# Moving the streamed operands of a 256-token block kernel to other places modulo 512 bytes

## The reference, cut to what matters

```python
# first block
xn = rms_norm(h, norm1_g)
proj = xn @ w_in                                 # 1024 -> 5136, cut into twelve pieces
for n, y in enumerate((y_a, y_b, y_c, y_d)):     # each (256, 512), made from the pieces
    merged += sigmoid(xn @ w_gate[n] + b_gate[n]) * (y @ w_branch[n])
h = h + merged @ w_out
h = h + square(relu(rms_norm(h, norm2_g) @ w_ff1)) @ w_ff2         # 1024 -> 4096 -> 1024
h = h + sigmoid(rms_norm(h, norm3_g) @ w_ple_gate + b) * (p @ w_ple)
x = rms_norm(h, final_g)
# second block, shift/scale/gain from c @ ada_w
z = modulate(rms_norm_2(x, norm1_g), sh1, sc1) @ w_in + b_in       # 1024 -> 5640
merged = sigmoid(ga) * (ym @ p_mlstm) + sigmoid(gb) * (ya @ p_moba)
x = x + g1 * (merged @ w_out)
f = silu(h2 @ w_gate) * (h2 @ w_up)                                # 1024 -> 2816
x = x + g2 * (f @ w_down)
return rms_norm_2(x, normf_g)
```

## Time and profile before

| | us |
|---|---|
| median of 3 runs | 926.76 |
| lowest and highest | 924.8, 931.33 |
| the profiled execution | 926.27 |
| its span, first to last instruction | 925.0 |

### The profile page before, as it was taken

One profiled execution on the slowest core, in us unless ns is written; L12 is line 12 of the kernel. 1 busy time (PEld: TensorE's weight loads), 2 busy tenths in 40 slices (PEclk: granted clock), 3 DMA queues, 4 the chain that ended last, 5 costly groups with the idle time before them and its releaser, 6 DMA issues.

```text
span 925.0 us, 18432 instructions
## 1 busy us (share of the span) xinstructions
PE 896.8 (97%) x7356; PEld 869.6 (94%) x7356; DVE 729.2 (79%) x1146; ACT 565.3 (61%) x819; POOL 1.9 (0%) x9
## 2 busy tenths in 40 slices
PE   7999999999999999999999999999999999999995
PEld 6999989998999999999999989998989999999995
DVE  6778989979888899888965988968779885555554
ACT  7848366675576676654446778557685664445452
POOL 0000000000000000000000000000000000000000
PEclk9999999999999999999999999999999999999998
DMA  8766545556774789998855565553435656666641
GB/s 309 250 195 222 157 151 165 162 181 216 262 252 160 251 289 344 336 319 301 320 181 181 159 194 183 161 153 120 151 125 179 203 169 198 190 200 193 192 143 46
DMA packets 52533, 188.78 MB, mean 204 GB/s; under 512 B 5968, under 2 KB 6240, under 8 KB 52320
## 3 DMA queue, kind: packets, MB, share of 16 engines
q1 hardware_dynamic: 52304, 187.60, 61.4%
q10 hardware_dynamic: 144, 0.00, 0.0%
HBM read 186.53 MB, written 1.05 MB: 203 GB/s over the span
## 4 chain that ended last, share of the span: by engine, by line
PE 81%; DVE 12%; ACT 6%; issue 1%; DMA 0%; SPq 0%; DVEq 0%; ACTq 0%
PE bank L991 23%; PE bank L993 23%; PE bank L994 23%; DVE wlo L1024 3%; ACT whi L1817 2%; PE bank L965 1%; PE bank L967 1%; PE bank L966 1%; DVE cv L1098 1%; DVE hsc L1502 1%; DVE scr L1197 1%; PE bank L696 1%; ACT P L1928 1%; DVE stat L1229 1%; DVE Alo L1059 1%
## 5 line engine op out<-in xcount | busy, mean ns | idle before, releaser
L1024 DVE TENSOR_TENSOR wlo<-raw,whi 128x1024 fp32r<-128x1024 f32 x297 | 361.3, 1222 | 121.2 <-ACT whi L1817 120.8
L1817 ACT ACTIVATE whi<-raw 128x1024 fp32r<-128x1024 f32 x297 | 311.7, 1056 | 207.9 <-PE bank L994 191.3
L991 PE MATMUL bank<-Alo,whi 128*128 128x256 f32 x1376 | 388.3, 282 | 2.5 <-ACT Ahi L1837 1.4
L993 PE MATMUL bank<-Ahi,wlo 128*128 128x256 f32 x1376 | 382.6, 278 | 0.0
L994 PE MATMUL bank<-Ahi,whi 128*128 128x256 f32 x1376 | 382.6, 278 | 0.0
L991 PEld LDWEIGHTS bank<-Alo,whi 128*128 128x128 f32 x1376 | 259.2, 188 | 7.3 <-issue 4.1
L994 PEld LDWEIGHTS bank<-Ahi,whi 128*128 128x128 f32 x1376 | 259.5, 189 | 0.0
L993 PEld LDWEIGHTS bank<-Ahi,wlo 128*128 128x128 f32 x1376 | 258.7, 188 | 0.6 <-issue 0.2
L993 PE MATMUL bank<-Fhi,wlo 128*128 128x256 f32 (+1 forms) x288 | 81.1, 282 | 0.0
L994 PE MATMUL bank<-Fhi,whi 128*128 128x256 f32 (+1 forms) x288 | 81.1, 281 | 0.0
L991 PE MATMUL bank<-Flo,whi 128*128 128x256 f32 x256 | 72.2, 282 | 0.0
(11 more groups left out here) (391 smaller groups left out, 1355.4 us busy)
## 6 DMA issues: line engine op xcount, KB each, us to landing
raw<-in_stream SPq DMA_DIRECT2D x297, 512.0 KB, 4.2
araw<-in_ada SPq DMA_DIRECT2D x48, 512.0 KB, 6.3
TB<-in_TB SPq DMA_DIRECT2D x1, 1536.0 KB, 7.6
H<-in_xT SPq DMA_DIRECT2D x4, 256.0 KB, 5.3
out<-H SPq DMA_DIRECT2D x4, 256.0 KB, 2.2
bc<-in_bc SPq DMA_DIRECT2D x1, 896.0 KB, 5.8
raw<-in_stream SPq DMA_DIRECT2D x2, 256.0 KB, 4.4
mats<-in_mats SPq DMA_DIRECT2D x1, 449.0 KB, 9.1
```

The source lines that it names most:

```text
L991: pe.matmul(os[j], wh, xl, start=k == 0 and (wide or j == 0), stop=False, skip_group_check=not wide)
L993: pe.matmul(os[j], wl, xh, start=False, stop=False, skip_group_check=not wide)
L1024: v.tensor_tensor(wlo[:, s % NHL, :], raw[:, s % NRAW, :], whi[:, s % NHL, :].bitcast(F32), ALU.subtract).then_inc(*lo_v.up(s))
L1817: a.activation(whi[:, s % NHL, :], raw[:, s % NRAW, :], ACT.Copy).then_inc(*hi.up(s))
```

## The change

Five unused tiles are added or resized. They hold nothing and no instruction names them; each one pushes the tiles behind it in its region. `gap1` (128 bytes) at the head of `p1`, `gap2` (256) at the head of `p2`, `gap3` (384) at the head of `p3`, `gap4` (384, in place of the old `gap3` of 576) in the middle of `p3`, `gap5` (320) at the head of `p4`.

```diff
@@ -301,6 +300,7 @@
         p1 = ExitStack()
         s1 = lambda name, shape, dt=F32: sb(name, shape, dt, p1)
+        s1("gap1", [128, 32])
         TB = s1("TB", [128, 8, 384])
@@ -336,6 +336,7 @@
         p2 = ExitStack()
         s2 = lambda name, shape, dt=F32: sb(name, shape, dt, p2)
+        s2("gap2", [128, 64])
         Fhi = s2("Fhi", [128, 32, T], F32R)
@@ -358,11 +359,12 @@
         p3 = ExitStack()
         s3 = lambda name, shape, dt=F32: sb(name, shape, dt, p3)
+        s3("gap3", [128, 96])
         Mhi, Mlo = s3("Mhi", [128, 8, T], F32R), s3("Mlo", [128, 8, T], F32R)
 
         mv = s3("mv", [128, 2, 512])
         mo = s3("mo", [128, 4, T])
-        s3("gap3", [128, 144])
+        s3("gap4", [128, 96])
         bc2 = s3("bc2", [128, 512])
@@ -395,6 +397,7 @@
         p4 = ExitStack()
+        sb("gap5", [128, 80], F32, p4)
         Uhi = sb("Uhi", [128, NF2, T], F32R, p4)
         Ulo = sb("Ulo", [128, NF2, T], F32R, p4)
```

## The result

The changed kernel took 931.61 us (median of 20 runs, 929.07 to 938.04) against 924.95 us (median of 20, 923.59 to 931.33): 6.7 us more, a ratio of 1.0072 with a 95% interval of 1.0057 to 1.0086. The forecast was 925.0 us, 1.3 us less than the profiled execution before. The time lies within the range of 914 to 938 us and within 1%, but it moved the other way. The profiled execution after took 930.11 us, its span is 928.8 us; it lies 1.5 us under its median, and the one before 1.3 us over its own (of 20), so the two traces differ by 3.8 us only.

The account below looks back on a forecast made before the run. TensorE, busy 97% of the span, bounds the kernel by matmul count times pace. F, B and Ya gain 2.4 us, U gives back 0.9 and M 0.2: net -1.3 from the profiled 926.27, so 925.0 us, range 914 to 938.

Parts of the forecast that it names:

- The two levels of 113.4 and 117.7 ns: Long matmul stretches: U at the lower pace, F at the upper, normed products at both, at full clock.
- nothing would show in the waits or in DMA: VectorE and ScalarE have idle time, costed at nothing; TensorE waits growing over 3 us would refute the forecast.
- the test: Group means of F, U, M and Y: F at 276 a gain, U at 281 a loss, above 281 rival B.
- rival B: Moved F, U, M and Y products go at the wide products' 122.4 ns: 15.4 us slower, 941.7 us, chance 0.20.
- a third pace outside 113 to 118 ns: Sign that the forecast is wrong: moved products starting at a pace outside 113 to 118 ns.
- the value I take is what the unmoved tile shows over the whole run: Moved products take the normed tile's average pace, 0.4 of it upper: 115.1 ns.
- the place alone does not choose the level: F, U and the normed operand shared one place modulo 512 yet ran at different levels, 113.4 and 117.7 ns.
- 528 x 1.7 = 0.9 us: U's products, at the lower level before, give back 0.9 us by going to the average pace.
- The gain of 2.4 us in F, B and Ya: Their 912 products, all at the upper level, go from 117.7 to 115.1 ns, gaining 2.4 us.
- Rival A: The old distance is bad for everything; moved products reach the transposes' 110 ns: 15.4 us gained, 910.9 us, chance 0.15.
- Rival D: Places of the moved tiles don't matter, so the change does nothing: 926.3 us, chance 0.10.
- may take its level with them: Normed products following a moved one without a break may take its level, either way: nothing on the average.

Follow-up runs that it names:

- before_again: The kernel before, unedited, run and profiled a second time: 925.9 us against 926.09, ratio 0.9991.
- all_up320: Kernel before plus an unused 320-byte tile ahead of raw, moving every tile up and keeping all distances from the weights: 924.28 us against 925.21, ratio 0.9986.
- f_only: Kernel before with gap2 alone, F and B at distance 192 from the weights: 924.88 us against 926.3, ratio 0.9986.
- p3_only: Kernel before with the new gap3 and gap4 alone, M at distance 320, shifted, Ya and Ym at 128: 926.1 us against 926.3, ratio 0.999.
- u_only: Kernel before with gap5 alone, U at distance 256 from the weights: 929.87 us against 926.3, ratio 1.0029.
- y_only: Kernel before with gap1 alone, Y and the first block's work tiles 128 bytes on, Y at distance 64: 929.28 us against 926.3, ratio 1.0032.
- after_u_back: Changed kernel without gap5, U back at distance 448: 934.36 us against 926.09 for the kernel before, ratio 1.0074.
- u_back_2: Same program as after_u_back (changed kernel without gap5), run again for a profile: 925.49 us, beside 925.33 us for the kernel before.

## Why the prediction was wrong

**What held.** The kernel is a count of matmuls times a pace, and everything that moved is in that pace. The two levels of 113.4 and 117.7 ns, and that nothing would show in the waits or in DMA, were right. F, U, M and Y were named as the test, and U's mean of 283 is what rival B was to show (above 281). The forecast also named a third pace outside 113 to 118 ns as the sign that it is wrong, and U's 120.0 ns is that sign. That the time lies within the range all the same is luck: only U, 528 of 6,624 products, was put at such a distance.

**What failed is the value taken for a new place.** The step was "the value I take is what the unmoved tile shows over the whole run", 115.1 ns for F, B, Ya, U and M. It rested on "the place alone does not choose the level", which was true of one distance and said nothing of others: in the trace before all operands had the same distance, so there was no row on any other. At distance 256 U went at 120.0 ns. That term was 528 x 1.7 = 0.9 us and measured 528 x 6.7 = 3.5 us. The gain of 2.4 us in F, B and Ya did not exist: 192 is the same place as 448 by the repeat of 256 bytes, so F could not change, and B went with it; Ya went to 118.7 ns. So the forecast of 1.3 us less became 6.7 us more. The term had been made by letting a group at its upper level fall back to a mean, as if the level were drawn for it, but in every trace with F at 192 or 448, twelve of them, F is at 117.8 ns throughout.

**Rival B was right in kind** for U: it had 122.4 ns there and 4.8 us, against 120.0 ns and 3.5 us. It was wrong in reach: M and Y have, at 320 and 64, only the old levels in other shares. Its total of 15.4 us would have needed all moved tiles at such a place; in the kernels at distances 0 and 256 all tiles are, the normed one too, which costs 24 us. Its 122.4 ns was also read from a window with a break in it, two matmuls of another kind:

```profile
735.27 0.59 PE L554 MATMUL bank<-nrm,ones 128*128 128x256 f32 x2
```

Without that break the wide products before start every 120.9 ns, near the 120.0 ns that U came to.

Rival A did not occur at any distance: nothing narrow went below 113 ns for long, and the transposes' 110 ns were no bound that this stream reaches. Rival D, the rule of the Trainium skill ("TensorE: Matmul & The Clock Gate", "Step-by-step: what each phase is for") that the load of the next weights takes nothing from the stream, does not hold in the use made of it here, that places don't matter: with the same instructions, the distance of the streamed operand from the weights changes the pace from 113.3 to 120.0 ns.

**The other 3 us.** A part of them is Y. There are six traces with Y at 448 whose normed operand is at 448 too (before, before_again, all_up320, f_only, p3_only, u_only) and five with Y at 64 (y_only, after and the three of after_u_back). Of the Y distances 226 are upper on the average in the six and 483 in the five. The normed operand did not move, but up to 312 us, while Y is in use, it has 282 to 465 upper ones in the six and 742 to 804 in the five. These ranges are far apart, so this is no draw: it belongs to Y's place or to that of a tile moved with it. Behind 312 us, where no Y is left, the two ranges overlap (727 to 1,076, and 624 to 1,206), and a difference there is one of draws. The forecast had this step, "may take its level with them", and priced it at nothing on the average.

Not every slower product reaches the total. By the counts, 257 Y and 390 normed distances of 4.4 ns make 2.8 us, but before some breaks TensorE then waits less. From matmul to matmul, the stretch from 38 to 84 us is 1.0 to 1.1 us longer with Y at 64, and the one from 133 to 312 us 0.7 us on the average (179.5 to 180.1 us against 178.1 to 179.4). Between the two lies the stretch in which the clock falls in some executions; where it did not, Y makes no difference there. That is 1.8 us for Y in all, close to the 1.9 us by which the lower times of y_only lie over those of before. By what path Y's place acts on products of another tile is not shown.

**p3** cost nothing that the total of its run shows. Ya's and Ym's 118.7 to 119.4 ns is a new pace of their own; the wide products start every 122 ns in four of the five traces with the new place and every 120.7 in the fifth (120.5 to 120.9 in the six with the old). In the traces, the stretch between 680 and 747 us, which holds them and M, is 0.5 us longer on the average of the five with the new place than of the six without (0.1 to 0.9 us over before, against 0.0 to 0.4).

Together with U's 3.5 us this makes an estimate of 5.8 us, of 6.7 measured. The last 1 us is open. It is less than the 2.3 us that one stretch differed by between two executions of one program, and the slower group of runs, 5 to 8 us up, was never profiled.

## What to carry to other kernels

When a kernel is a stream of weight loads and matmuls with little else, measure the pace from start to start per operand, and try the address of the streamed tile against that of the weights before anything else: here it was worth 25 us of 925 between the best and the worst place, with no instruction changed. A trace in which all operands have one relation to each other can't price another relation; then the forecast has to go by bounds and not by a mean. And when levels are drawn, two profiles of the same program come before an explanation of the difference between two programs.

## What the runs showed of the hardware that was not expected

- The pace of a stream of 128 x 128 fp32r weight loads and 256-column matmuls depends on the distance of the streamed operand's address from that of the weights' tiles within a partition: 113.3 ns at best, 120.0 ns at distances 0, 96, 128 and 256 for U. Moving all tiles by 320 bytes left U at 113.3 ns.
- The two pairs that lie 256 bytes apart (0 and 256, 192 and 448) have the same paces, with the same count of matmuls in the windows from 478, 775 and 870 us.
- At some distances there are two stable paces for the same instructions, 113.3 and 117.8 ns. A stretch keeps its pace until other work on TensorE interrupts it or the stream goes over to another tile: in the eleven traces with the normed operand at 448, all but a few of the 283 changes of level are at such a point. Which level it takes is mostly a matter of the program and sometimes of the execution, and up to 312 us it changes with the place of a tile that the stretch doesn't stream. At distances 0 and 256 there is one pace only.
- The granted clock falls in some executions between 105 and 120 us, where small matmuls of the scan (64 columns and 64 partitions, L637) break up the products: over these 15 us it was 1.00 in 12 of the 20 profiled executions, 0.89 in seven and 0.77 in one (y_only). From 84 to 133 us the four with 0.89 and the normed operand at 448 take 49.6 to 50.0 us, u_only and u_back_2, at 1.00 and with about as many products at each pace, 48.4 us, and y_only 51.4 us. It happens at all kinds of distances.
